# Expert layers of a transformer: first weights split during the output projection, bounds and masks on POOL, gather over eight banks, combine tile by tile

## The reference

```
xt = rms_norm(h, ln_ffn)
g_prob = softmax(xt @ w_group + b_group)          # 4 groups, the best one
e_prob = softmax(logits of that group's 8 experts) # the two best, e_w made to sum to 1
comb = g_w * e_w;  cw = one-hot sum over (token, expert)   # 256 x 32, two entries a row
hid = silu(xt @ w_gate[e]) * (xt @ w_up[e])        # 32 experts, 1024 -> 128
h = h + sum over e of (hid * cw[:, e]) @ w_down[e] # 128 -> 1024
gate = sigmoid(rms_norm(h, ln_ple) @ ple_w_gate)
h = h + gate * (p @ ple_w_proj)                    # the embedding
```

## Time and profile before

| | us |
|---|---|
| median of 3 runs | 1210.54 (1205.42 to 1211.98) |
| the profiled execution | 1211.84 |
| its span | 1210.1 |
| PE busy | 1090.7 (90%) |
| DVE busy | 763.8 (63%) |
| ACT busy | 720.8 (60%) |
| POOL busy | 72.2 (6%) |
| mean granted clock of PE | 0.946 of full speed |

### The profile page before, as it was taken

One profiled execution on the slowest core, in us unless ns is written; L12 is line 12 of the kernel. 1 busy time (PEld: TensorE's weight loads), 2 busy tenths in 40 slices (PEclk: granted clock), 3 DMA queues, 4 the chain that ended last, 5 costly groups with the idle time before them and its releaser, 6 DMA issues.

```text
span 1210.1 us, 17394 instructions
## 1 busy us (share of the span) xinstructions
PE 1090.7 (90%) x6140; PEld 905.5 (75%) x6140; DVE 763.8 (63%) x1331; ACT 720.8 (60%) x1228; POOL 72.2 (6%) x111
## 2 busy tenths in 40 slices
PE   5968889999999997899979999978979969999988
PEld 4857677999998785797667777747868767787756
DVE  4536664666665665456567778765755467778864
ACT  4435664444443544385649888835656549988834
POOL 9000600000000012000100000000000100000000
PEclk9987699999999999899989999998989979999998
DMA  9784003665654545002507999853601607999830
GB/s 291 182 206 151 1 10 126 212 191 177 191 187 147 178 139 186 2 2 87 209 25 255 327 322 329 308 169 112 191 15 36 261 3 258 338 328 335 305 138 35
DMA packets 105083, 210.79 MB, mean 174 GB/s; under 512 B 7992, under 2 KB 49816, under 8 KB 104752
## 3 DMA queue, kind: packets, MB, share of 16 engines
q1 hardware_dynamic: 101984, 204.04, 49.4%
q0 software_dynamic: 2736, 4.80, 2.2%
q10 hardware_dynamic: 288, 0.99, 0.2%
HBM read 207.17 MB, written 2.62 MB: 173 GB/s over the span
## 4 chain that ended last, share of the span: by engine, by line
PE 79%; DVE 8%; ACT 5%; issue 3%; DMA 3%; SPq 1%; DVEq 1%; ACTq 0%
PE bank L794 22%; PE bank L1501 13%; PE bank L1518 9%; PE bank L1186 8%; PE bank L1196 7%; PE bank L889 4%; PE bank L870 2%; PE bank L713 2%; PE bank L878 2%; DMA expert_w<-in_moe_w_up 1%; PE bank L869 1%; PE bank L1995 1%; PE bank L1342 1%; ACT x_high L767 1%; DMA ring<-in_w_uq 1%
## 5 line engine op out<-in xcount | busy, mean ns | idle before, releaser
L794 PE MATMUL bank<-weight_parts,x_high 128*128 128x512 f32 (+3 forms) x832 | 252.1, 389 | 27.9 <-issue 15.5
L794 PEld LDWEIGHTS bank<-weight_parts,x_high 128*128 128x128 f32 x832 | 159.6, 199 | 59.1 <-issue 21.9
L1501 PE MATMUL bank<-expert_high,block_high 128*128 128x256 f32 x560 | 183.7, 328 | 2.5 <-issue 2.4
L815 DVE TENSOR_TENSOR weight_parts<-ring,weight_parts 128x1024 fp32r<-128x1024 f32 (+3 forms) x108 | 121.1, 1140 | 93.7 <-ACT weight_parts L812 93.6
L812 ACT CAST weight_parts<-ring 128x1024 fp32r<-128x1024 f32 (+3 forms) x108 | 103.8, 983 | 122.0 <-PE bank L794 95.1
L1438 DVE TENSOR_TENSOR expert_low<-expert_w,expert_high 128x1024 fp32r<-128x1024 f32 x140 | 164.9, 1218 | 11.7 <-ACT expert_high L1431 11.5
L794 PE MATMUL bank<-weight_parts,x_low 128*128 128x512 f32 (+3 forms) x416 | 160.2, 385 | 0.0
L1501 PE MATMUL bank<-expert_low,block_high 128*128 128x256 f32 x560 | 158.5, 283 | 0.0
L1501 PE MATMUL bank<-expert_high,block_low 128*128 128x256 f32 x560 | 158.5, 283 | 0.0
L1431 ACT CAST expert_high<-expert_w 128x1024 fp32r<-128x1024 f32 x140 | 140.2, 1054 | 14.3 <-DMA expert_w<-in_moe_w_up 13.9
L1518 PE MATMUL bank<-expert_w,junk 128*128 128x512 f32 x280 | 132.1, 595 | 2.6 <-DVE arena L1574 1.4
(11 more groups left out here) (330 smaller groups left out, 1732.2 us busy)
## 6 DMA issues: line engine op xcount, KB each, us to landing
expert_w<-in_moe_w_gate SPq DMA_DIRECT2D x70, 512.0 KB, 5.6
expert_w<-in_moe_w_up SPq DMA_DIRECT2D x70, 512.0 KB, 7.1
expert_w<-in_moe_w_down SPq DMA_DIRECT2D x70, 512.0 KB, 5.4
ring<-in_w_ff SPq DMA_DIRECT2D x64, 512.0 KB, 3.9
ring<-in_w_in SPq DMA_DIRECT2D x16, 512.0 KB, 11.6
ring<-in_a_w_in SPq DMA_DIRECT2D x16, 512.0 KB, 4.8
ring<-in_ple_w_gate SPq DMA_DIRECT2D x16, 512.0 KB, 5.5
ring<-in_w_o SPq DMA_DIRECT2D x8, 512.0 KB, 6.3
```

The costliest lines, as they stand in the source:

```text
L794: mm = nc.tensor.matmul(bank[:, j["m"] % 4, 0:n], j["operand"][x][:, 2 * c + kk, at[0]:at[1]], weight_parts[:, number % PAIRS, w, kk * n:( ...
L815: nc.vector.tensor_tensor(low, raw_weights, high, ALU.subtract).then_inc(weights_split, 1)
L1501: mm = nc.tensor.matmul(bank[:, 4 + b % 2, 0:256].rearrange("p (q n) -> p q n", q=2), x[:, b % 2, k, :], w[:, k], start=k == 0 and n == 0, ...
```

## The change

- The weights of experts 0 and 1 are cast on ACT after its last piece of the output projection, and split on DVE between the projection's second and third addition to `h`. `expert_high` moves from the end of the ring to the place of the attention's result (`mix`), `place_turned` and the embedding's product move too.
- The embedding product of token tile 1 is done after the places, and in banks 0 and 3.
- DVE makes `cw` directly after the router, ahead of the slots.
- ACT copies the bounds of the experts' slots to SBUF; POOL computes `home`, `strays` and both masks from them (`pool_steps`), with additions, multiplications and a clamp to 0..1 in place of comparisons, and with sums by halving. The tile numbers of eight experts are packed in one number, which an engine loads and takes apart with shifts.
- The gather uses all eight banks, so the second half waits for no split. The shares go to bank 6, are copied to SBUF by ACT, and POOL reads them there.
- DVE copies the low part of x for blocks 0 and 1.
- In the combine all four tiles are done as high and low. A tile is rounded and split when it is complete: tile 0 within the loop, tile 1 before the last addition. The sums go to banks 4 to 7, and DVE adds each piece to `h` when its own bank is done.

The core of the diff (declarations, tables and the two removed functions' bodies are cut):

```diff
     def pe_gather(pe, layer):
...
         for half in range(2):
+            if half:
+                pe.wait_ge(embed_taken, 4 * (layer + 1))
+                pe.wait_ge(bounds_kept, layer + 1)
             for k in range(4 * half, 4 * half + 4):
-                if half:
-                    pe.wait_ge(sorted_split, KB * layer + k - 3)
                 for t in range(TILES):
-                    nc.tensor.matmul(bank[:, k % 4 + 4, :], by_chunk(high_rows, t)[:, k, :], place[:, t, :],
+                    nc.tensor.matmul(bank[:, SORT_BANKS[k], :], by_chunk(high_rows, t)[:, k, :], place[:, t, :],
...
     def tiles_of(eng, b):
-        _, tiles = nc.values_load_multi_w_load_instructions(steps_i[0:1, b:b + 8], engines=[eng.engine], min_val=0,
-                                                            max_val=SORT_TILES - 1)
-        return tiles
+        packed = eng.value_load(steps_i[0:1, b // 8:b // 8 + 1], min_val=0, max_val=4 ** 8 - 1)
+        return [(packed >> 2 * j) & 3 for j in range(8)]
...
     def pe_combine(pe, layer):
-        pe.wait_ge(ex_added, BLOCKS * (layer + 1))
-        for t in range(TILES):
-            for half in range(2):
-                nc.tensor.matmul(bank[:, 2 * t + half, :], place_turned[:, 0, t * P:(t + 1) * P].bitcast(F32),
-                                 acc[:, half * 512:(half + 1) * 512], start=True, stop=False)
-        for q in range(1, SORT_TILES):
-            pe.wait_ge(acc_split, (SORT_TILES - 1) * layer + q)
+        for q in range(SORT_TILES):
+            pe.wait_ge(acc_split, SORT_TILES * layer + q + 1)
...
         for b in range(BLOCKS):
             hid(b)
-            if b >= 3:
+            if 3 <= b < BLOCKS - 1:
                 add(b - 3)
+            if b == BLOCKS - 1:
+                add(BLOCKS - 3)
             if b + 2 < BLOCKS:
                 dve_split_expert(dve, layer, b + 2)
-        for b in range(BLOCKS - 3, BLOCKS):
-            add(b)
...
+            if b == BLOCKS - 2:
+                add(BLOCKS - 4)
+                split_acc(0)
+        add(BLOCKS - 2)
+        split_acc(1)
+        add(BLOCKS - 1)
+        split_acc(2)
+        split_acc(3)
...
+    def pool_steps(pool, layer):
...
+        pool.wait_ge(bounds_kept, layer + 1)
+        def positive(x):
+            link(g.tensor_scalar(x, x, 0.0, 1.0, ALU.max, ALU.min))
+
+        def fold(x, total, n):
+            while n > 2:
+                n //= 2
+                link(g.tensor_tensor(x[:, :, 0:n], x[:, :, 0:n], x[:, :, n:2 * n], ALU.add))
+            return g.tensor_tensor(total, x[:, :, 0], x[:, :, 1], ALU.add)
+
+        passed = reached[:, 1:SORT_TILES]
+        g.tensor_tensor(passed, over(starts, EXTRA), along("below", EXTRA), ALU.subtract)
+        link(g.tensor_tensor(beyond, over(ends, EXTRA), along("edge", EXTRA), ALU.subtract))
+        positive(passed)
+        positive(beyond)
+        link(g.tensor_tensor(home[:, :], passed[:, 0], passed[:, 1], ALU.add))
+        link(g.tensor_tensor(home[:, :], home[:, :], passed[:, 2], ALU.add))
+        link(g.tensor_tensor(packed[:, :], home[:, :], table_of("pack"), ALU.mult))
+        link(fold(packed[:, :].rearrange("p (w j) -> p w j", w=4), words[:, 0:4], 8))
+        g.tensor_copy(steps_i[:, 0:4], words[:, 0:4])
...
+        link(fold(extras, strays[:, :], EXPERTS))
+        g.tensor_copy(steps_i[:, EXPERTS:EXPERTS + EXTRA], strays[:, :]).then_inc(steps_ready, 1)
+        g.tensor_tensor(mask_a, along("next", SORT_TILES), over(starts, SORT_TILES), ALU.subtract)
...
+        pool.wait_ge(shares_kept, layer + 1)
+        link(g.tensor_tensor(mask_a, mask_a, shares[:, :, :], ALU.mult))
...
+        fold(extras, extra_w[:, :], EXPERTS).then_inc(masks_ready, 1)
...
     def pe_moe_and_ple(pe, layer):
...
-        pe_embed(pe, layer)
+        pe_embed(pe, layer, 0)
         pe_places(pe, layer)
-        pe.wait_ge(embed_taken, 4 * (layer + 1))
+        pe_embed(pe, layer, 1)
+        pe.wait_ge(embed_taken, 4 * layer + 2)
         pe_gather(pe, layer)
...
         take_linear(act, l_nsa_o, "act")
+        act_cast_expert(act, 0, 0)
+        act_cast_expert(act, 0, 1)
...
-        take_linear(dve, l_nsa_o, "dve")
+        take_linear(dve, l_nsa_o[0:2], "dve")
+        dve_split_expert(dve, 0, 0)
+        dve_split_expert(dve, 0, 1)
+        take_linear(dve, l_nsa_o[2:], "dve")
```

More of the change, by code:

```diff
@@ L48 @@
 for _name, _width in (("place", SORTED), ("before", 128), ("ones", 128), ("first", 64), ("bounds", 64), ("expert", 32),
[L49 removed]
+                      ("rank", 32), ("pack", 32), ("below", EXTRA), ("next", SORT_TILES), ("edge", EXTRA), ("extra", EXTRA), ("slot", SORT_TILES), ("tile", SORT_TILES)):
     ROUTE[_name] = (_at, _width)
@@ L71, in route_table @@
     put("rank", EXPERTS - e[None])
+    put("pack", 4.0 ** (e % 8)[None])
+    put("below", 128.0 * np.arange(1, EXTRA + 1)[None] - 1)
+    put("next", q + 1 + 128.0 * np.arange(SORT_TILES)[None])
     put("edge", 128.0 * np.arange(1, EXTRA + 1)[None])
@@ L1367, in pe_places @@
                          skip_group_check=True)
-        nc.tensor.matmul(bank[:, 2, 64:128], counts[:, :], table_of("bounds", EXPERTS), start=True, stop=True,
+        nc.tensor.matmul(bank[:, 1, 64:128], counts[:, :], table_of("bounds", EXPERTS), start=True, stop=True,
                          skip_group_check=True).then_inc(slots_made, 1)
@@ L1577, in dve_experts @@
         tiles = []
-        dve_split_expert(dve, layer, 1)
-        dve_masks(dve, layer)
+        dve.wait_ge(steps_ready, layer + 1)
+        tiles.extend(tiles_of(dve, 0))
+        dve.wait_ge(sorted_split, KB * (layer + 1))
+        for b in range(2):
+            v.tensor_copy(block_low[:, b % 2], sorted_low[:, :, ds(tiles[b] * P, P)]).then_inc(ex_copied_low, 1)
+        dve.wait_ge(masks_ready, layer + 1)
         dve.wait_ge(acc_zeroed, layer + 1)
@@ L1633, in dve_masks @@
-        link(v.tensor_tensor(by_second, picks[:, 1], wide(c1(58), EXPERTS), ALU.mult))
-        v.tensor_tensor(cw[:, :, :], by_first, by_second, ALU.add).then_inc(cw_ready, 1)
-        in0, in1 = (scratch[:, 256 + i * 128:384 + i * 128].rearrange("p (q e) -> p q e", q=SORT_TILES) for i in (0, 1))
-        v.tensor_tensor(in0, over(starts, SORT_TILES), along("slot", SORT_TILES), ALU.is_le)
-        link(v.tensor_tensor(in1, over(ends, SORT_TILES), along("slot", SORT_TILES), ALU.is_gt))
-        link(v.tensor_tensor(in0, in0, in1, ALU.mult))
@@ L1640, in dve_masks @@
-        dve.wait_ge(shares_made, layer + 1)
-        link(v.tensor_tensor(in0, in0, bank[:, 3, 0:128].rearrange("p (q e) -> p q e", q=SORT_TILES), ALU.mult))
-        link(v.tensor_tensor(in1, over(home[:, :], SORT_TILES), along("tile", SORT_TILES), ALU.is_equal))
-        link(v.tensor_tensor(in1, in1, in0, ALU.mult))
-        link(v.tensor_reduce(home_w[:, :], in1.rearrange("p q e -> p e q"), AX.X, ALU.add))
-        in1 = scratch[:, 0:96].rearrange("p (x e) -> p x e", x=EXTRA)
-        link(v.tensor_tensor(in1, over(home[:, :], EXTRA), along("extra", EXTRA), ALU.is_lt))
```

194 lines of the change are left out of this document (108 added, 86 removed).

## The result

The changed kernel takes 1175.39 us (median of 4 runs, 1173.07 to 1180.3) against 1210.3 before: ratio 0.9717, 95% interval 0.9687 to 0.9746. The forecast was 1182, range 1175 to 1198. A second set of five runs (e10) gave 1176.56 and 0.9711. The profiled execution has a span of 1173.2 us against 1210.1.

A forecast was written before the change was run, and what follows sets the result against it. PE was taken as the bound, with slack ahead of and behind the experts. Layer 1 gains 15.4 us and layer 2 13.8, together 29.2, from 1211.8 profiled to 1182.6; forecast 1182 us, range 1175 to 1198.

The forecast's parts named there:

- The start: Routing up to the first expert: expert 0 starts at 618.1 instead of 628.1; 10.5 us per layer, bounds 7 and 11.
- the forecast's reading of one DVE queue: Ahead of the experts: DVE's place, sorted_low, expert 1 split and cw, in order, hold PE until 623.07 in layer 1.
- Early splits in layer 2: Output projection: last two adds wait for expert 1's weights and split; cost 1.65 us, bounds 0 and 2.5.
- Steps: POOL's first 20 instructions, up to steps_ready: 7.0 us, ready at 609.4, needed at 615.
- the bound of 11.7: POOL's steps: collisions with six DVE instructions may stretch POOL by 4.7 us beyond 7.0, steps at 614.1, still in time.
- masks: POOL's last 11 instructions, behind the shares: 4.2 us, ready at 622.5.
- The cover: POOL's masks before expert 2: masks up to 623.2 cost nothing, 0.7 us of cover.
- its sign: Sign of being right: POOL's last mask comes within 2 us of gate_up(0)'s end.
- The rivals in which POOL decides: Routing: POOL late at twice the price, 1197 us, chance 12%; or POOL the bound and kernel slower, 1232 us, 5%.
- The loop: Expert loop: fewer DVE adds held in issue by tile-number loads; -0.5 us per layer, bounds 0 and -1.5.
- The tail: Combine, last expert matmul to last h add: 8.8 us instead of 13.2; -4.4 per layer, bounds -3.5 and -5.
- rival 3: Experts: DMA takes the gain back, 4 to 5 us a layer lost in later weights, 1191 us; chance 10%.

The follow-up runs named there:

- e10: The changed kernel run and profiled again with no edit: 1176.56 us, ratio 0.9711 to the kernel before.
- e9: Changed kernel with experts 0 and 1 cast and split in the routing, and bounds and masks on DVE: 1184.42 us, ratio 0.9781 to before.
- e5: Changed kernel with 12 more linked POOL multiplies of 128x32 between the shares and the masks: 1186.68 us, ratio 0.9807 to before.
- e2: Changed kernel with eight tile numbers loaded every eight experts instead of one packed word: 1190.94 us, ratio 0.9842 to before.
- e1: Changed kernel with the old combine, all adds after the loop and tile 0 in plain fp32: 1186.59 us, ratio 0.9807 to before.
- e3: Changed kernel with experts 0 and 1 cast and split in the routing, not the output projection: 1181.97 us, ratio 0.9774 to before.
- e11: Changed kernel with layer 2's expert 1 split moved, DVE copying expert 2's low block and splitting its first half early: 1180.0 us, ratio 0.9727.

## Why the prediction was right, and where it was off

**The start: right.** 9.87 us in layer 1 against 10.0 forecast, 10.4 against 10.5 to gate_up(2), and the parts as described: tile 1 partly at half clock, the gather and shares at full, 0.5 us in which PE waits for the first block copy (0.7 forecast). In layer 2 the start gained 11.0 and 11.6 to gate_up(2). The experiments say what carried it. Undone alone, in layer 1: splits 1.9, banks 1.0, chain 0.2 (1.2 in layer 2), packed load 2.0. But splits and chain together cost 4.0: each hides behind the other, so that no single part is worth what the forecast's reading of one DVE queue gave it. What lies between e9's 28.0 and the old 33.9 (banks, load, `cw` ahead of the shares, which PE then ran 2.6 us faster with the flip) was undone only in part: `cw`'s place was never undone, so its share of the gain is argued, not shown.

**Early splits in layer 2: right**, 1.4 us late against 1.65 forecast. The forecast missed that a wait there moves the half clock to where it does not hurt: 1.0 of the 1.4 comes back.

**POOL: the mechanism right, the price low.** Steps took 9.6 us, not 7.0, by collisions (a 128x32 multiply of 1.12 us beside DVE's x split, 0.33 with its link in e5's dose) and a dearer tensor_scalar (0.6 to 0.7 us), within the bound of 11.7; masks 4.1 against 4.2. The cover was 0.2 to 0.4 us, not 0.7 (e5), and the last mask came 2.2 us behind gate_up(0)'s end, a little outside the 2 us that the forecast named as its sign. The rivals in which POOL decides did not occur, but were near: the dose shows 3.9 us on POOL costing 5.2 and 4.8 us a layer with the clock.

**The loop: the mis-sized term.** "-0.5 us per layer, bounds 0 and -1.5" measured -3.3 and -1.5, in layer 1 outside its bound. The row of "issue" was read rightly, but PE's losses were taken from too few places: e2 gives 2.4 and 1.4 of it back, and PE's waits there are for the additions that stand in "issue" and for ACT's copies of `hidTs`, which the forecast did not count.

**The tail:** 4.8 against 4.4; e1 returns 4.65.

**The clock behind the experts** was in no term: before, both gates began at half clock (0.57, 0.50), after, neither did in the first profile. That is worth 1.6 to 2.8 us a gate, and by e10 it is chance.

**The number.** The profiled pair differs by 36.9 us where the forecast had 29.2. Over the forecast lie the loop (3.8 us), the start of layer 2 (1.1), the tails (0.8), the additions (0.3) and the clock of the two gates (4.2); the later start of layer 1 takes 2.5 back. So luck is 1.7 us of the pair. The medians differ by 34.9 us, and that lies in the range without it: the start and the combine were sized rightly, the loop too small.

**DMA took nothing back** (rival 3): share 0.95 in the loop, and e5, e2 and e3 pass a late start on undiminished.

## To carry to other kernels

Undo parts in pairs as well as alone: where two works share a queue with slack, each looks free. Price an idle stretch of the matmul engine twice, as idle time and as half clock behind it, and look whether independent matmuls fit into it. Registers loaded one by one inside a loop can hold the bound engine through the engine that waits for them: undone alone, packing eight numbers into a word cost 12.4 us by the stages (e2), the combine 9.3 (e1), the early splits 9.0 (e3).

## What the runs showed of the hardware

- A POOL operation stretches two to five times beside DVE, DVE hardly: the fold 1.18 to 2.18 us in e11 and a small cast 0.19 to 1.05 us in e3, while DVE's splits beside them took their usual 1.2; in e3 a 128x128 multiply took 1.49 us instead of 0.47 beside DVE's plain copy, which has one input and took 1.29, as without POOL. DVE's first two `place` passes took 0.99 us beside POOL and 0.88 without it.

```profile
616.58 1.49 POOL L1692 TENSOR_TENSOR probT<-probT,shares 128x128 f32<-128x128 f32 x1 [3.25 <-ACT shares L1480]
```

```profile
616.46 1.29 DVE L1610 CAST block_low<-sorted_low 128x1024 fp32r x2
```

The Trainium skill, "SBUF — State Buffer", section "SBUF: two separate sides", has the lock also for DVE operations in a two-port mode, not only for those with two SBUF inputs. These rows are consistent with that, though no row says in which mode the copy ran. The prediction counted six DVE instructions that meet POOL's chain, and no plain copy among them.

- PE's idle time ahead of the gate was the same in all ten profiles with the new combine and no fillers (1.22 us, transposes, 3.41 us), in both layers; the gate began at full clock in 6 of these 20 and at half clock in 14. What decides it, no run here shows.
- Twenty chained POOL operations on small tiles took 9.6 us where the same on DVE took 4.4 (606.10 to 610.5 in e9), so POOL is a second queue, not a fast one. Part of the 9.6 us are collisions with DVE.
